# A ScalarE activation moved ahead of the weight casts, and a small transpose moved one weight block forward

## The reference, cut to what matters

```
# block 1, mixer: z = h @ w_in, cut into conv input a, gate g, q, k, v and f_logit (8 columns, one a head)
u = silu(layer_norm(causal_depthwise_conv(a * sigmoid(g), conv_w) + conv_b))     # 31 taps
log_f = log_sigmoid(f_logit + b_forget)
att = forgetting_attention(q, k, v, log_f)            # softmax(q k^T / 8 + cumulative sums of log_f) v
y = concat([u, att]) @ w_out
# block 1, memory attention: keys and values come from rms_norm(mem) @ w_mk and w_mv

# block 2, mixer: proj = n @ w_in_2, cut into z, xbc, dt_raw and the three short-conv parts
xbc = silu(causal_dwconv(xbc, conv_ssd_w) + conv_ssd_b)                          # 4 taps
xs, Bm, Cm = split(xbc)
y = ssd_scan(xs, softplus(dt_raw + dt_bias), -exp(a_log), Bm, Cm) ...
y = y * silu(z)
```

## Time and profile before

| | |
|---|---|
| median of three runs | 1466.16 us |
| lowest, highest | 1465.92, 1467.77 us |
| profiled execution, its time | 1465.92 us |
| its span in the trace | 1464.2 us |
| granted PE clock, mean | 0.993 |
| PE busy | 1410.2 us (96%) |
| DVE busy | 1090.7 us (74%) |
| ACT busy | 786.4 us (54%) |
| POOL busy | 65.3 us (4%) |
| chain that ended last, by engine | PE 82%; DVE 13%; ACT 3%; issue 1% |

### The profile page before, as it was taken

One profiled execution on the slowest core, in us unless ns is written; L12 is line 12 of the kernel. 1 busy time (PEld: TensorE's weight loads), 2 busy tenths in 40 slices (PEclk: granted clock), 3 DMA queues, 4 the chain that ended last, 5 costly groups with the idle time before them and its releaser, 6 DMA issues.

```text
span 1464.2 us, 25691 instructions
## 1 busy us (share of the span) xinstructions
PE 1410.2 (96%) x8505; PEld 1244.4 (85%) x8505; DVE 1090.7 (74%) x2073; ACT 786.4 (54%) x1287; POOL 65.3 (4%) x63
## 2 busy tenths in 40 slices
PE   7989889999899998999999999999999999999998
PEld 7867778888799887889999999888888888878886
DVE  6897766666778678489989998566666666677776
ACT  6644865555667534455555554455555555545544
POOL 0200000000000522010000000000000000000000
PEclk9999999999999999999999999999999999999999
DMA  7442426566345513454556887656657575577754
GB/s 291 157 131 87 144 90 197 187 187 196 124 153 166 170 68 102 171 189 145 201 176 227 258 254 255 215 189 223 216 186 254 188 244 197 190 236 250 250 194 143
DMA packets 103353, 274.56 MB, mean 188 GB/s; under 512 B 8176, under 2 KB 41072, under 8 KB 102784
## 3 DMA queue, kind: packets, MB, share of 16 engines
q1 hardware_dynamic: 64832, 237.11, 48.7%
q10 hardware_dynamic: 38176, 34.63, 7.3%
q0 software_dynamic: 288, 2.10, 0.5%
HBM read 254.93 MB, written 18.87 MB: 187 GB/s over the span
## 4 chain that ended last, share of the span: by engine, by line
PE 82%; DVE 13%; ACT 3%; issue 1%; DMA 0%; POOL 0%; DVEq 0%; ACTq 0%
PE Y L1910 42%; PE AO L1910 37%; DVE wl L1018 3%; DVE CV L1118 2%; PE M L1910 2%; ACT wh L484 1%; DVE I L1567 1%; DVE X L1238 1%; DVE SCO L1583 1%; DVE I L1581 1%; ACT xhl L529 0%; DVE V L1589 0%; DVE V L1575 0%; DVE xn L1235 0%; PE M L2260 0%
## 5 line engine op out<-in xcount | busy, mean ns | idle before, releaser
L1018 DVE TENSOR_TENSOR wl<-raw,wh 128x1024 fp32r<-128x1024 f32 x440 | 543.1, 1238 | 202.1 <-ACT wh L484 201.6
L1910 PE MATMUL AO<-xhl,wh 128*128 128x256 f32 (+3 forms) x2784 | 649.6, 316 | 3.6 <-DVE wl L1018 2.0
L484 ACT CAST wh<-raw 128x1024 fp32r<-128x1024 f32 x440 | 461.1, 1050 | 154.0 <-PE Y L1910 80.5
L1910 PEld LDWEIGHTS AO<-xhl,wh 128*128 128x128 f32 x2784 | 456.2, 189 | 36.0 <-DVE wl L1018 2.2
L1910 PE MATMUL AO<-xhl,wl 128*128 128x256 f32 (+2 forms) x1776 | 485.1, 282 | 0.0
L1910 PEld LDWEIGHTS AO<-xhl,wl 128*128 128x128 f32 x1776 | 334.2, 188 | 7.9
L1910 PE MATMUL Y<-wh,peer_ah 128*128 128x512 f32 x512 | 199.4, 389 | 3.1 <-DVE peer_al L1715 3.1
L1910 PE MATMUL Y<-wh,peer_al 128*128 128x512 f32 x512 | 199.2, 389 | 0.0
L1910 PE MATMUL Y<-wl,peer_ah 128*128 128x512 f32 x512 | 199.2, 389 | 0.0
L936 ACT CAST peer_ah<-hid 128x256 fp32r (+1 forms) x128 | 52.0, 406 | 181.2 <-DVE hid L1709 95.9
L1910 PEld LDWEIGHTS Y<-wh,peer_ah 128*128 128x128 f32 x512 | 96.2, 188 | 21.4 <-DVE peer_al L1715 2.3
(11 more groups left out here) (322 smaller groups left out, 1598.5 us busy)
## 6 DMA issues: line engine op xcount, KB each, us to landing
raw<-in_stream SPq DMA_DIRECT2D x440, 512.0 KB, 3.3
gate_spill<-gstage ACTq DMA_DIRECT2D x32, 512.0 KB, 5.0
gates<-gate_spill ACTq DMA_DIRECT2D x6, 2048.0 KB, 15.0
gates<-gate_spill ACTq DMA_DIRECT2D x8, 512.0 KB, 7.1
rowg<-in_post SPq DMA_DIRECT2D x3, 512.0 KB, 4.3
X<-in_x SPq DMA_DIRECT2D x2, 512.0 KB, 4.7
memx<-in_mem SPq DMA_DIRECT2D x1, 1024.0 KB, 7.7
keys<-in_keys POOLq DMA_DIRECT2D x1, 1024.0 KB, 6.9
```

The costliest lines, as they stand in the source:

```text
L484: nc.scalar.copy(wh[:, s, :], raw[:, s, :]).then_inc(split_hi, 1)
L1018: nc.vector.tensor_tensor(wl[:, s, :], raw[:, s, :], wh[:, s, :].bitcast(F32), ALU.subtract)\
L1910: return nc.tensor.matmul(o, a, b, start=start, stop=stop)
```

## The change

Three edits.

- In the mixer of block 2, ACT's Silu of the fifth `xbc` group, with its wait for all 80 tap instructions, stands straight behind the loop over the groups, ahead of the first cast of stage `z`. It stood behind the third `turned_out`.
- In stage `qk`, PE's `thin_turn` stands behind qk0 instead of qk1, and writes to `M[:, 0, 0:16]` instead of `Y[:, 1, 0:16]`. Since `mem_part` overwrites that bank, PE waits for `f_z` (DVE has read it) behind qk2; the wait for `f_z` at the start of the attention goes.
- In the same stage DVE's `forget(0)` stands behind the five taps of block 1 instead of ahead of them, and reads from `M`.

```diff
             xbc_groups(3, XBC_T // 4)
+            act.wait_ge(xconv, 4 * XBC_T)
+            nc.scalar.activation(XS[:, XBC_T - 4:, :], XS[:, XBC_T - 4:, :], ACT.Silu).then_inc(xsilu, 1)
...
                 if j < len(turned):
                     turned_out(j)
-                if j == 2:
-                    act.wait_ge(xconv, 4 * XBC_T)
-                    nc.scalar.activation(XS[:, XBC_T - 4:, :], XS[:, XBC_T - 4:, :], ACT.Silu).then_inc(xsilu, 1)
...
-                    step(nc.vector.tensor_tensor(zf, Y[:, 1, 0:16].rearrange("p (j h) -> p j h", j=TT),
+                    step(nc.vector.tensor_tensor(zf, M[:, 0, 0:16].rearrange("p (j h) -> p j h", j=TT),
...
                 split(STREAM["qk"] + 4, j)
+                some_taps(3 if 2 <= j < 6 else 5)
                 if j == 1:
                     forget(0)
-                some_taps(3 if 2 <= j < 6 else 5)
...
                 wide("qk", j, xh, xl, T)
-                if j == 1:
-                    thin_turn(0, [(Y[:, 1, 8 * k:8 * k + 8], P, P * k) for k in range(TT)], FOX_H).then_inc(f_prod, 1)
+                if j == 0:
+                    thin_turn(0, [(M[:, 0, 8 * j:8 * j + 8], P, P * j) for j in range(TT)], FOX_H).then_inc(f_prod, 1)
+                if j == 2:
+                    pe.wait_ge(f_z, 1)
...
             pe.wait_ge(norm_lo, 4)
-            pe.wait_ge(f_z, 1)
             pe.wait_ge(dec_done, 3)
```

## The result

| | before | after |
|---|---|---|
| median of the runs (lowest to highest), us | 1467.08 (1465.92 to 1469.73), 8 runs | 1476.13 (1472.67 to 1479.19), 8 runs |
| profiled execution, us (its span) | 1465.92 (1464.2) | 1476.14 (1474.4) |
| mean granted clock of it | 0.993 | 0.988 |

The changed kernel is slower: ratio 1.006, 95% interval 1.0051 to 1.0069. That is 9.05 us between the medians, where the forecast was 7.3, and the time lies 0.5 us above the upper end of the range. It is nearest to the rival "all three fall" (1475.8). The base has moved too: the median of before is 1467.08 over eight runs, 0.9 us above that of the three runs which the forecast was built on. The two profiled executions are 10.2 us apart, since that of before happened to be the fastest of its runs; what follows is the working of that pair, and then how much of it other executions bear out.

A forecast was written before the change was run, and what follows sets the result against it. PE was taken to bound stage z, and DVE, reached through ACT, stage qk. Waits of 2.2 and 2.6 us plus 2.5 for clock falls made 7.3 us, or 1473.3 us; range 1470.4 to 1475.6.

The forecast's parts named there:

- all three fall: Rival: the clock falls behind all three new PE gaps, 4.8 us besides the waits; 1475.8 us, chance 0.17.
- Part 1: Stage qk: PE's transposes behind qk0 wait 2.3 us for ACT's copy `thin_t`, starting at 43.06; DVE comes 2.2 us late.
- Part 2: Stage qk: PE waits 2.1 us for `f_z` at the memory transposes, hidden beside ACT's table loads, costing nothing.
- Part 3: Stage z: the early Silu holds ACT, so PE's third transposition waits 2.6 us for its bank, paid in full.
- The sum of the waits: 2.2 us in stage qk plus 2.6 in stage z, 4.8 us, without any clock effect.
- Part 4: PE's granted clock falls behind one to two of the three new gaps, adding 2.5 us; bounds 0 and 4.8.
- The forecast's own chances and prices: Falls behind the three new gaps, in order: chances 0.6, 0.5 and 0.7; costs 1.7, 1.4 and 1.7 us.
- The time without any fall: Rival: the clock falls behind none of the new gaps, leaving only waits of 4.8 us; 1471.0 us, chance 0.10.

The follow-up runs named there:

- e5: Changed kernel with matmuls of no use filling PE's three new waits; 1471.13 us, ratio 1.0023 to the kernel before.
- e11: Changed kernel run again unchanged, for a second profile; 1476.74 us, ratio 1.0065 to the kernel before.
- e3: e2 with `forget(0)` put back ahead of the five taps; 1470.20 us, ratio 1.0016 to the kernel before.
- e1: Kernel before with the Silu edit alone; 1470.95 us, ratio 1.0026.
- e10b: e8 run once more, as common base for e9 and e10; 1465.10 us, ratio 0.9979 to the kernel before.
- e9: Changed kernel with matmuls of no use in seven PE waits, the three new and four old; 1469.37 us, ratio 1.0012 to the kernel before.
- e4: Kernel before with only `forget(0)` late and its wait at the memory transposes, `thin_turn` left behind qk1; 1469.41 us, ratio 1.0011.
- e6: e1 with matmuls of no use filling its gap in stage z; 1468.10 us, ratio 1.0003 to the kernel before.
- e7: e2 with matmuls of no use filling its two gaps in stage qk; 1469.86 us, ratio 1.0011 to the kernel before.
- e2: Kernel before with the stage qk edits alone, Silu left in its old place; 1472.59 us, ratio 1.0032.
- e10: e1 with its stage z gap and the four old gaps filled with matmuls of no use; 1466.71 us, ratio 0.9995 to the kernel before.
- e8: Kernel before with matmuls of no use in four old PE gaps, at three norms and near 580 us; 1464.04 us, ratio 0.9976.

## Why the prediction was wrong, step by step

- **Part 1, the first stand: right in place, short by 0.1 to 0.6 us.** Forecast 43.06, measured 43.13 in the first profile, but 43.70 in e5 and e11 (44.44 in e3). `thin_t` stands behind ACT's memory scaling, which waits for POOL's `stat` and began between 39.14 (e1) and 40.61 us (e3), differently in each execution. In the old order the 0.81 us for which ACT waits for qk1 takes that in: in e10b the scaling began at 39.97, 0.75 later than in before, and the DVE row of 53.72 stands at 53.82. In the new order PE waits for it.
- **Part 2, the second stand "hidden, with nothing to spare": nearly.** At the full clock (e9) ACT waits 0.20 us for qk3, and DVE is 2.97 us late instead of 2.25. The parts are 2.25, the 0.47 by which ACT's scaling began later in e9 (39.69), and the 0.20. Alone, the late `forget(0)` moves DVE by 0.65 us (e4).
- **Part 3, the stall in z: right.** 2.65 us in the profile for 2.6; in the time 1.6 to 2.4 on the common base, and 0.25 in e6, where a fall is missing further on.
- **The sum of the waits, 4.8 us: right within the noise.** 4.3 or 4.8 (e9 against e10b), and 3.3 in e5, which lacks the same fall as e6.
- **Part 4, "between one and two falls, 2.5 us": this is the step that failed.** The price of each was right within 0.4 us: 1.66, 1.74 and 1.4 us for 1.7, 1.4 and 1.7. The count was wrong: three in the first profile, two and one at another place in the second. Where 2.5 us were put down, taking the three gaps away saves 5.0 us (e5), although PE then works more. The forecast's own chances and prices would have given 2.9 us on average. These chances, 0.5 to 0.7 a gap, rested on two old gaps that fell and one that didn't, ordered by length, and length isn't what decides: 2.11 with a fall and 2.10 without at the same place, 2.49 without one at 110 us, and the old gap of 2.72 without one in e11. What decides it is open.
- **What I left out.** How long the clock stays low at the old places isn't the same in every execution (the 0.7 us behind the norm at 396 us), and whether it falls there isn't either. A change that only shifts these places may move the time by that; the profiles are too few to show it. And the forecast took the profile of before as typical; it was the fastest of its eight runs, with no fall at 1282 us, where eight of the twelve experiments' profiles have one.

The range was too narrow at the top for the same reason: it ended just under three falls at 4.8 us and allowed nothing for falls elsewhere, nor for the base. Of the 2.8 us between 1473.3 and 1476.13, 0.9 is the higher median of before, and 1.8 is the change itself (9.05 for 7.3).

The time without any fall was to be 1471.0, and the changed kernel reached it only with the gaps filled, in e5 (1471.13) and, with the old gaps filled too, in e9 (1469.37). The Trainium skill (TensorE: Matmul & The Clock Gate, HAM oscillation) warns only of longer gaps than these; the falls behind gaps of 2.12, 2.11 and 2.49 us in the first profile go against it.

## What to carry to other kernels

Where the bounding engine is TensorE, a wait of 2 us in a stretch that was dense cost here not 2 us but up to 3.7: look at the granted clock behind the gaps of that size which the kernel already has, and price the new one with a fall unless several executions say otherwise. An operation that is moved ahead of its neighbour "to be early" should be checked against when its input is ready: here both moves put a wait for something 2 to 5 us away in front of work that was ready. And matmuls of no use in a gap that can't be removed are a cheap test of what the clock costs, and sometimes a gain (3 us here on the kernel before).

## What the runs showed of the hardware that I had not expected

- Added up over slices of half a microsecond, the lower level lasted 3.4 us each time, or twice that, apart from the last one at the program's end. It was 6.8 us behind the norm at 396 us after the change and in e1 to e5, e7 and e11, behind the norm at 207 us after the change and in e2, and at 43 and 98 us in e3.
- The same instructions with the same gap in front of them meet either level in different executions: at 1282 us behind a gap of 1.88 us there was no fall in the profiles of before, of the change, of e3, e5, e10 and e10b, and one in those of e1, e2, e4, e6 to e9 and e11. One fall where PE bounds is worth some 1.7 us, so this may be a good part of the 3.8 us over which the kernel before spreads (which of its executions had it isn't recorded), and a difference of 1 to 2 us from a pair of profiles says nothing by itself.
- A fall doesn't need a long gap. In e5, e6 and e8 the clock fell at 579.5, 575.9 and 571.9 us beside gaps of 1.0 and 0.8 us, and in e6 and e8 at 630.5 and 626.5 us, 1.6 to 2 us behind the old gap of 1.64 that had none in the profile of before.
- Filling one gap can move a fall instead of removing it (583 to 571.9 us in e8).
